# A hybrid attention trunk on one core: a fifth k pair of the output projection as 2x2 block products

## The chip, the core and the metric

One core of a Trainium2 chip runs the whole program. The metric is device time in microseconds (us), the median of three runs. The engines are TensorE (PE in the profile, its weight loads PEld), VectorE (DVE), ScalarE (ACT), GpSimd (POOL) and SyncE (SP), which issues most DMA transfers.

## The reference

Two layers over x of 512 tokens by 2048 features, in float32. Each layer does

```
h = rmsnorm(x, norm_g)
aq, ak, av, ag, bq, bk, bv, bg = split(h @ w_in)         # 2048 x 6400
ya = chunked attention with relative bias (16 heads) * silu(ag)
yb = sliding window attention, rope, sinks (16 heads, 2 kv) * silu(bg)
x  = x + concat(ya, yb) @ w_out                          # 2048 x 2048
```

and a last rmsnorm follows. The change concerns `concat(ya, yb) @ w_out`, mostly, and the tables of rope and bias.

## The kernel before

Everything is kept transposed: features on the 128 partitions, the 512 tokens along the free axis. A projection makes output tiles of 128 features; each sums over 16 k tiles. To keep float32 accuracy with the fast matmul type, each operand is split into a high and a low part, and each product is three matmuls: high weights by high activations, high by low, low by high. ScalarE copies the raw weights into the high part (`hi_place`, or `split_w` in the plain tiles), VectorE subtracts to make the low part (`lo_place`), and TensorE waits for it (`w_lo_done`). The activations' parts are `act_hi` and `act_lo`.

The output projection of a layer has 16 output tiles. Tiles 0 to 3 are made one by one (`project`). From there they are made in pairs, o = 2 to 7 in layer 0 and 2 to 6 in layer 1 (`SUM_FIRST`, `SUM_END`), 11 pairs in all; the last two tiles of layer 1 are plain again. In a pair, the 8 k pairs (two k tiles by two output tiles, a 2x2 block of weights, against the two k tiles of activations, of which each is cut into left and right tokens) are "chunks" of two kinds. A "p" chunk is 12 matmuls of 512 columns (`plain_products`, L800 to L805). An "s" chunk does the 2x2 block product in seven instead of eight products (`sum_products`, L787 to L789): 21 matmuls of 256 columns. It needs sums of weights (`sum_w`, four VectorE ops on 128x128 blocks that make 7 blocks out of 4) and sums of activations. These are made once a layer, in place in `xy` (`sum_y`, four VectorE ops), and split into high (`hi_y_sums`, two ScalarE copies) and low (`lo_y_sums`, two VectorE ops).

`CHUNKS` is the order of the chunks in a pair: s0 s1 p0 s2 s3 p1 p2 p3. The raw, high and low weight buffers hold 32 blocks. `place(i)` says where chunk i lies: the s chunks take turns in two places of 7 blocks, the p chunks have four places of 4 blocks behind them. SyncE's `load_place(l, o, i, lows)` loads a chunk (256 KB) when so many low parts are done; `exchange(l, o)` loads the two residual tiles of a pair and stores two finished tiles of x. At the end of a pair VectorE combines the products (`sum_of_products`, L1604 to L1613) and, once TensorE has finished the pair, adds them and the residual into x (`add_products`, L1619); `residual` (L1559) does that for plain tiles. The squares of the new x are summed up on the side (`square` L1031, `sum_odd` L1687, `sum_even`).

Each engine runs a fixed order of work written by hand, and semaphores tie them. The order around the first pair of a layer is in `out_sums` of ScalarE and of VectorE. At the layer's end, layer 1's tiles 0 and 1 are made with alternating quarters; their inputs are copied by ScalarE while the last pair of layer 0 is still being multiplied, as `rows_done` tells which rows of `act_hi` and which weights are free:

```
if L > 0 and c < PTS - 1:
    act.wait_ge(rows_done, L * ROWS_LAYER - ROWS_OUT + ROWS_IN + 2 + c)
copy(w_hi[:, 1, chunk(c)], w_raw[:, 1, chunk(c)]).then_inc(w_hi_second, 1)
```

`strips` holds the bias of one pair of heads, loaded before each pair of the first mixer (`load_strips`), with one corner set by a memset once at the start; `cos_sb` and `sin_sb` are rope's tables, loaded once and read by GpSimd's `rope`.

## Time and profile before

| what | value |
|---|---|
| median of 3 runs | 1628.84 us (1628.83 to 1628.99) |
| profiled execution | 1628.75 us, of which the span shown is 1627.0 us |
| mean granted TensorE clock | 0.998 |
| TensorE busy | 1615.4 us, 8182 matmuls |
| VectorE, ScalarE, GpSimd busy | 1060.9, 875.2, 93.5 us |
| layer 0's first pair starts (first L787) | 684.28 us |
| layer 1's first pair starts | 1485.93 us |

The profile is of one execution. A time in a timeline is the instruction's start from the span's start; the number behind it is its length. Consecutive instructions of one engine overlap a little in their records, so what an instruction costs its engine is read from start to start. A busy TensorE is a stream of matmuls whose records overlap as well.

### The profile page before, as it was taken

The numbers are of one execution on the slowest core, as the hardware profiler recorded it, in microseconds if no ns is written. First come the engines' busy times: TensorE is split into PE (matmuls) and PEld (weight loads), VectorE is DVE, ScalarE is ACT, GpSimd is POOL, SyncE is SP. The second block draws the span as 40 slices with busy tenths as digits, with TensorE's granted clock in tenths as the row PEclk, the third lists the DMA queues.
The fourth block names the chain that finished last, engine by engine and source line by source line (L and its number), as shares of the span: only waits on it lengthen the run. The fifth ranks groups of instructions, "written<-read, shape, count | busy, mean of one in ns | idle before, by whom it ended". The sixth has DMA issues, their size and how long they took to land.

```text
span 1627.0 us, 23808 instructions
## 1 busy us (share of the span) xinstructions
PE 1615.4 (99%) x8182; PEld 1370.8 (84%) x8182; DVE 1060.9 (65%) x2378; ACT 875.2 (54%) x1907; POOL 93.5 (6%) x74
## 2 busy tenths in 40 slices
PE   9999999999999999999999999999999999999997
PEld 7888888888888888899888888888888888888997
DVE  7655555555577777777755555555556677787765
ACT  7555655555646666333545555655546466653333
POOL 0000000000121200000000000000002212000000
PEclk9999999999999999999999999999999999999999
DMA  7232222232322322444432232222232323223443
GB/s 253 90 104 101 89 78 89 90 115 75 104 93 91 104 98 91 137 145 149 140 129 79 89 115 90 89 77 89 96 109 89 100 91 104 91 91 123 130 136 117
DMA packets 49724, 173.75 MB, mean 107 GB/s; under 512 B 6464, under 2 KB 10848, under 8 KB 35696
## 3 DMA queue, kind: packets, MB, share of 16 engines
q1 hardware_dynamic: 49184, 172.16, 31.6%
q8 instruction: 41, 0.67, 0.2%
q10 hardware_dynamic: 432, 0.55, 0.1%
q14 instruction: 35, 0.29, 0.1%
q0 software_dynamic: 32, 0.08, 0.0%
HBM read 159.58 MB, written 8.47 MB: 103 GB/s over the span
## 4 chain that ended last, share of the span: by engine, by line
PE 99%; DVE 0%; DMA 0%; DVEq 0%; ACT 0%; issue 0%; ACTq 0%
PE ps_proj L581 23%; PE ps_proj L583 23%; PE ps_proj L582 23%; PE ps_o L648 2%; PE ps_t L638 2%; PE ps_o L800 1%; PE ps_o L804 1%; PE ps_o L805 1%; PE ps_proj L800 1%; PE ps_proj L804 1%; PE ps_proj L805 1%; PE ps_s L630 1%; PE ps_s L629 1%; PE ps_o L688 1%; PE ps_s L663 1%; PE ps_o L581 1%
## 5 line engine op out<-in xcount | busy, mean ns | idle before, releaser
L581 PE MATMUL ps_proj<-act_hi,w_hi 128*128 128x512 f32 x1632 | 643.8, 394 | 0.0
L583 PE MATMUL ps_proj<-act_hi,w_lo 128*128 128x512 f32 x1632 | 637.7, 391 | 0.0
L582 PE MATMUL ps_proj<-act_lo,w_hi 128*128 128x512 f32 x1632 | 636.5, 390 | 0.0
L1285 DVE TENSOR_TENSOR w_lo<-w_raw,w_hi 128x512 fp32r<-128x512 f32 (+1 forms) x528 | 380.1, 736 | 176.3 <-ACT w_hi L898 174.1
L898 ACT ACTIVATE w_hi<-w_raw 128x512 fp32r<-128x512 f32 (+1 forms) x528 | 330.9, 649 | 128.3 <-DVE w_raw L1593 61.9
L583 PEld LDWEIGHTS ps_proj<-act_hi,w_lo 128*128 128x128 f32 x1632 | 306.3, 188 | 66.6
L582 PEld LDWEIGHTS ps_proj<-act_lo,w_hi 128*128 128x128 f32 x1632 | 306.9, 188 | 57.4
L581 PEld LDWEIGHTS ps_proj<-act_hi,w_hi 128*128 128x128 f32 x1632 | 306.6, 188 | 57.7
L964 ACT ACTIVATE probs<-probs,nmax 128x128 f32<-128x128 f32 (+3 forms) x128 | 72.1, 563 | 109.8 <-DVE nmax L1357 106.7
L898 ACT ACTIVATE probs<-probs,rden 128x128 f32<-128x128 f32 (+3 forms) x128 | 72.1, 563 | 106.7 <-DVE rden L1378 106.7
L898 ACT ACTIVATE arena<-ps_t 128x512 fp32r<-128x512 f32 (+4 forms) x168 | 74.6, 448 | 68.3 <-PE ps_t L674 50.5
L1285 DVE TENSOR_TENSOR arena<-ps_t,arena 128x512 fp32r<-128x512 f32 (+4 forms) x168 | 85.0, 510 | 37.7 <-ACT arena L898 36.4
L1297 DVE SCALAR_TENSOR_TENSOR temp<-ps_proj,rstd 128x512 f32<-128x512 f32 x94 | 64.5, 686 | 42.5 <-PE ps_proj L583 41.4
L898 ACT ACTIVATE temp<-ps_o 64x256 f32<-64x256 f32 (+1 forms) x96 | 43.3, 451 | 84.6 <-PE ps_o L648 62.2
L1357 DVE CUSTOM_DVE_ANT_0 probs<-ps_s,strips 128x256 f32<-128x256 f32 (+2 forms) x96 | 53.3, 555 | 49.5 <-PE ps_s L630 49.2
L1873 POOL TENSOR_TENSOR temp<-temp,cos_sb 128x512 f32<-128x512 f32 x18 | 24.1, 1338 | 955.2 <-DVE temp L1297 955.2
L1285 DVE TENSOR_TENSOR k_st<-temp,k_st 64x512 fp32r<-64x512 f32 x72 | 52.4, 728 | 31.1 <-ACT k_st L898 30.3
L981 ACT ACTIVATE probs<-probs,nmax 128x128 f32<-128x128 f32 (+1 forms) x128 | 49.1, 384 | 38.6 <-DVE nmax L1371 38.6
L1286 DVE SCALAR_TENSOR_TENSOR arena<-temp,arena 64x512 fp32r<-64x512 f32 x64 | 43.9, 686 | 25.2 <-ACT arena L898 24.2
L898 ACT ACTIVATE arena<-temp 64x512 fp32r<-64x512 f32 x64 | 40.3, 629 | 37.2 <-DVE temp L1297 23.5
L1031 ACT ACTIVATE temp<-xy 128x512 f32<-128x512 f32 x30 | 18.5, 631 | 75.7 <-DVE xy L1619 55.0
L638 PE MATMUL ps_t<-flip_sb,probs 128*128 128x128 f32 x320 | 56.2, 273 | 0.0
(264 smaller groups left out, 2203.1 us busy)
## 6 DMA issues: line engine op xcount, KB each, us to landing
w_raw<-w SPq DMA_DIRECT2D x107, 1024.0 KB, 4.8
w_raw<-w SPq DMA_DIRECT2D x98, 256.0 KB, 3.8
temp<-temp SPq DMA_DIRECT2D x72, 64.0 KB, 4.0
strips<-ext SPq DMA_DIRECT2D x16, 256.0 KB, 5.7
temp<-xT SPq DMA_DIRECT2D x16, 256.0 KB, 4.0
xs<-xy SPq DMA_DIRECT2D x16, 256.0 KB, 3.8
temp<-xs SPq DMA_DIRECT2D x16, 256.0 KB, 2.7
strips<-ext SPq DMA_DIRECT2D x16, 224.0 KB, 5.7
```

What stands on the lines that cost most here:

```text
L581: pe.matmul(dst, wh, act_hi[:, k, :], start=start, stop=False)
L582: pe.matmul(dst, wh, act_lo[:, k, :], start=False, stop=False)
L583: return pe.matmul(dst, wl, act_hi[:, k, :], start=False, stop=stop)
L638: mm = pe.transpose(ps_t[e % 2][:, kt * P:(kt + 1) * P], probs[:, e % 2, kt * P:(kt + 1) * P], flip_sb[:, :])
L648: mm = pe.matmul(ps_o[h][:, kt * P:SEQ], a_v[:, kt, h * P:(h + 1) * P], part[:, kt * (PT_STEP + P):kt * PT_STEP + SEQ], start=(kt == 0 and ...
L898: return nc.scalar.activation(dst, src, ACT.Copy, scale=scale)
L964: nc.scalar.activation(row, row, ACT.Exp, bias=nmax[:, e % 2, 0:1], scale=-1.0, accum_out=psum_e[:, e % 2, 0:1]).then_inc(exp_done, 1)
L981: nc.scalar.activation(row, row, ACT.Exp, bias=nmax[:, n % 2, b:b + 1], scale=-1.0, accum_out=psum_e[:, n % 2, b:b + 1])
L1285: return nc.vector.tensor_tensor(dst, src, hi, ALU.subtract)
L1286: return nc.vector.scalar_tensor_tensor(out=dst, in0=src, scalar=scale, in1=hi, op0=ALU.mult, op1=ALU.subtract)
L1297: nc.vector.scalar_tensor_tensor(out=dst, in0=(ps or ps_proj[s % 2])[:, :], scalar=scale, in1=rstd[:, :], op0=ALU.mult, op1=ALU.mult).then ...
L1357: nc.vector.tensor_tensor_reduce(out=probs[:, e % 2, 0:n], in0=ps_s[e % 2][:, 0:n], in1=bias, scale=-1.0, scalar=LOWEST, op0=ALU.add, op1= ...
```

## The change

Five of the eight k pairs are "s" chunks now (`SUM_K = 5`), and the order in a pair is s0 s1 s2 s3 s4 p0 p1 p2. The s chunks take turns in three places of 7 blocks; p0 and p1 lie behind them, and p2 lies in the third s place, behind its first 3 blocks. So s2's high part waits for the end of the pair before, and p2's for s2's products. The sums of activations of the fifth k pair need room: they take that of `strips`, `cos_sb` and `sin_sb`, which therefore are filled again in layer 1 (two transfers ahead of the first strips, and a memset). `sum_y(4)` and its parts are made within the first pair. At the end of layer 0, all quarters of layer 1's tile 1 are copied after the last pair.

```diff
@@ -61,17 +61,23 @@
 V_LAYER = PAIRS + 1
 ROPES = PAIRS + 1
-ROWS_IN, ROWS_OUT = PTS - 1, 4
+ROWS_IN, ROWS_OUT = PTS - 1, 3
 ROWS_LAYER = ROWS_IN + ROWS_OUT
 SUM_FIRST = 2
 SUM_END = (OUT_TILES // 2, OUT_TILES // 2 - 1)
-SUM_K = 4
-CHUNKS = (("s", 0), ("s", 1), ("p", 0), ("s", 2), ("s", 3), ("p", 1), ("p", 2), ("p", 3))
+SUM_K = 5
+CHUNKS = (("s", 0), ("s", 1), ("s", 2), ("s", 3), ("s", 4), ("p", 0), ("p", 1), ("p", 2))
 BLOCKS = 7 * P
 PLAIN = 4 * P
+N_PLAIN = KT // 2 - SUM_K
+SUM_PLACES = 3
+SUM_TURNS = tuple(len(range(p, SUM_K, SUM_PLACES)) for p in range(SUM_PLACES))
+PLAIN_FIRST = (SUM_PLACES * BLOCKS, SUM_PLACES * BLOCKS + PLAIN, SUM_PLACES * BLOCKS - PLAIN)
 W11, W12, S3, W22, S1, S2, S4 = range(7)
@@ -117,13 +123,17 @@
             return ctx.enter_context(nc.semaphore(name))
+        with nc.sbuf_tensor("strips_tables", [P, 4, SEQ], F32) as strips_tables:
+            strips = strips_tables[:, 0:2, :]
+            cos_sb, sin_sb = strips_tables[:, 2, :], strips_tables[:, 3, :]
+        y_sum_last = sb("y_sum_last", [P, 2, 2, SEQ], F32R)
         act_hi = sb("act_hi", [P, KT, SEQ], F32R)
         act_lo = sb("act_lo", [P, KT, SEQ], F32R)
         xy = sb("xy", [P, KT, SEQ])
         w_raw = sb("w_raw", [P, 2, KT * P])
         w_hi = sb("w_hi", [P, 2, KT * P], F32R)
         w_lo = sb("w_lo", [P, 2, KT * P], F32R)
-        strips = sb("strips", [P, 2, SEQ])
         arena = sb("arena", [P, ARENA], F32R)
         k_st = sb("k_st", [P, 2, 2, SEQ], F32R)
@@ -132,8 +142,6 @@
         temp = sb("temp", [P, 7, SEQ])
         rstd = sb("rstd", [P, SEQ])
         r_cols = sb("r_cols", [P, QT])
-        cos_sb = sb("cos_sb", [P, SEQ])
-        sin_sb = sb("sin_sb", [P, SEQ])
         eye_sb = sb("eye_sb", [P, P])
         flip_sb = sb("flip_sb", [P, P])
         ones_sb = sb("ones_sb", [P, 1])
@@ -248,8 +256,11 @@
         half_done = sem("half_done")
-        sum_in = [sem(f"sum_in{i}") for i in range(2)]
-        plain_in = [sem(f"plain_in{i}") for i in range(4)]
+        sum_in = [sem(f"sum_in{i}") for i in range(SUM_PLACES)]
+        plain_in = [sem(f"plain_in{i}") for i in range(N_PLAIN)]
+        strips_set = sem("strips_set")
+        tables_in = sem("tables_in")
         w_summed = sem("w_summed")
         multiplied = sem("multiplied")
         y_summed = sem("y_summed")
@@ -375,16 +386,19 @@
             kind, n = CHUNKS[i]
             if kind == "s":
-                return slice(n % 2 * BLOCKS, (n % 2 + 1) * BLOCKS)
-            return slice(2 * BLOCKS + n * PLAIN, 2 * BLOCKS + (n + 1) * PLAIN)
+                return slice(n % SUM_PLACES * BLOCKS, (n % SUM_PLACES + 1) * BLOCKS)
+            return slice(PLAIN_FIRST[n], PLAIN_FIRST[n] + PLAIN)
         def block_of(buf, n, b):
-            first = n % 2 * BLOCKS + b * P
+            first = n % SUM_PLACES * BLOCKS + b * P
             return buf[:, first:first + P]
         def y_sum(part, j):
             i, r = divmod(j, 2)
+            if i == 4:
+                return y_sum_last[:, part, r, :]
             buf = (k_f, v_st, arena, arena)[i]
             first = (2048 if i == 3 else 0) + (part * 2 + r) * SEQ
             return buf[:, first:first + SEQ]
@@ -466,8 +480,9 @@
                 sp.wait_ge(w_lo_done, (n - 2) * PTS + lows)
                 kind, c = CHUNKS[i]
                 first = place(i).start
-                sp.dma_start(raw_f[:, first:first + PLAIN], w[n + (kind == "p")][:, c * PLAIN:(c + 1) * PLAIN]
-                             ).then_inc((sum_in[c % 2] if kind == "s" else plain_in[c]), 16)
+                t, q = divmod(c if kind == "s" else SUM_K + c, PTS)
+                sp.dma_start(raw_f[:, first:first + PLAIN], w[n + t][:, q * PLAIN:(q + 1) * PLAIN]
+                             ).then_inc((sum_in[c % SUM_PLACES] if kind == "s" else plain_in[c]), 16)
             def load_out(l):
                 exchange(l, 1)
@@ -475,14 +490,15 @@
                     if o > SUM_FIRST:
                         exchange(l, o - 1)
-                    order = (((0, 4), (1, 4), (2, 8), (5, 8), (6, 8), (7, 8)) if o == SUM_FIRST else
-                             ((2, 3), (0, 4), (1, 5), (5, 6), (6, 7), (7, 8)))
+                    order = (((0, 2), (1, 4), (2, 6), (5, 7), (6, 8)) if o == SUM_FIRST else
+                             ((0, 4), (1, 5), (5, 6), (6, 7), (2, 8)))
                     for i, lows in order:
                         load_place(l, o, i, lows)
                     for par in range(2):
                         sp.sem_inc(w_in[par], 16)
                     load_place(l, o, 3, 9)
                     load_place(l, o, 4, 10)
+                    load_place(l, o, 7, 11)
                 exchange(l, SUM_END[l] - 1)
                 n = tile0(l) + IN_TILES + 2 * SUM_END[l]
                 for s, lows in ((0, 5), (1, 8)):
@@ -532,6 +548,9 @@
                 prefetch(T, 1)
                 for s in range(2, 4):
                     prefetch(T, s)
+                with sp.If(L > 0):
+                    for dst, src in ((cos_sb, cos), (sin_sb, sin)):
+                        sp.dma_start(dst[:, :], src).then_inc(tables_in, 16)
                 sp.wait_ge(ext_out, 16)
                 load_strips(L, 0)
                 with sp.Fori(1, PAIRS) as u:
@@ -799,12 +818,12 @@
                         cols = slice(first + (2 * r + k) * P, first + (2 * r + k + 1) * P)
                         mm = pe.matmul(dst, hi_f[:, cols], act_hi[:, row, :], start=False, stop=False, skip_group_check=True)
-                        if o == OUT_TILES // 2 - 1 and k == 0 and (r == 0 and j > 0 or j == 3):
+                        if o == OUT_TILES // 2 - 1 and k == 0 and r == 0:
                             mm.then_inc(rows_done, 1)
                         pe.matmul(dst, hi_f[:, cols], act_lo[:, row, :], start=False, stop=False, skip_group_check=True)
-                        mm = pe.matmul(dst, lo_f[:, cols], act_hi[:, row, :], start=False, stop=j == 3 and k == 1,
+                        mm = pe.matmul(dst, lo_f[:, cols], act_hi[:, row, :], start=False, stop=j == N_PLAIN - 1 and k == 1,
                                        skip_group_check=True)
-                if j < 3:
+                if j < N_PLAIN - 1:
                     mm.then_inc(multiplied, 1)
                 else:
                     mm.then_inc(proj_done, 2)
@@ -1043,12 +1062,12 @@
                 else:
                     act.wait_ge(plain_in[n], (nth(l, o) + 1) * 16)
-                if i < 3 and o == SUM_FIRST:
+                if i == 2 or i < 2 and o == SUM_FIRST:
                     act.wait_ge(proj_done, tile0(l) + IN_TILES + 2 * o + (i == 2))
-                elif i in (0, 1):
+                elif i < 2:
                     act.wait_ge(multiplied, nth(l, o - 1) * 7 + (4, 5)[i])
-                elif i in (3, 4):
-                    act.wait_ge(multiplied, nth(l, o) * 7 + (1 if i == 3 else 2))
+                elif i in (3, 4, 7):
+                    act.wait_ge(multiplied, nth(l, o) * 7 + {3: 1, 4: 2, 7: 3}[i])
                 copy(hi_f[:, place(i)], raw_f[:, place(i)]).then_inc(w_hi_done, 1)
             def out_sums(l):
@@ -1057,10 +1076,13 @@
                 for i in range(2):
                     hi_place(l, SUM_FIRST, i)
                 for o in range(SUM_FIRST, SUM_END[l]):
+                    hi_place(l, o, 2)
                     if o > SUM_FIRST:
                         square(l + 1, 2 * o - 2, o - 1, 0)
                     square(l + 1, 2 * o - 1, o - 1, 1)
-                    for i in range(2 if o == SUM_FIRST else 3, len(CHUNKS)):
+                    if o == SUM_FIRST:
+                        hi_y_sums(l, 4, 5)
+                    for i in range(3, len(CHUNKS)):
                         hi_place(l, o, i)
                     if o + 1 < SUM_END[l]:
                         hi_place(l, o + 1, 0)
@@ -1070,7 +1092,6 @@
                     copy(w1[:, 0:SEQ // 2], sum_banks(o)[1][0][:, 0:SEQ // 2]).then_inc(p1_copied, 1)
                     if o + 1 < SUM_END[l]:
                         hi_place(l, o + 1, 1)
-                        hi_place(l, o + 1, 2)
                 n = tile0(l) + IN_TILES + 2 * SUM_END[l]
                 act.wait_ge(w_in[0], n * 8 + 16)
                 for c in range(PTS):
@@ -1165,9 +1186,9 @@
                     if L < 1:
                         act.wait_ge(w_first[1][c], 16)
                     if L > 0 and c == 0:
                         act.wait_ge(w_in[1], 8 * TILES + 16)
-                    if L > 0 and c < PTS - 1:
-                        act.wait_ge(rows_done, L * ROWS_LAYER - ROWS_OUT + ROWS_IN + 2 + c)
+                        act.wait_ge(proj_done, T + 1)
                     copy(w_hi[:, 1, chunk(c)], w_raw[:, 1, chunk(c)]).then_inc(w_hi_second, 1)
                     if L < 1:
                         squares_first((c * KC + 1, c * KC + 3))
@@ -1583,7 +1604,7 @@
             def sum_w(l, o, n):
                 done = (nth(l, o) * SUM_K + n) * 4
-                dve.wait_ge(sum_in[n % 2], (nth(l, o) * 2 + n // 2 + 1) * 16)
+                dve.wait_ge(sum_in[n % SUM_PLACES], (nth(l, o) * SUM_TURNS[n % SUM_PLACES] + n // SUM_PLACES + 1) * 16)
                 b = [block_of(raw_f, n, i) for i in range(7)]
                 nc.vector.tensor_tensor(b[S1], b[S3], b[W22], ALU.add).then_inc(w_summed, 1)
                 dve.wait_ge(w_summed, done + 1)
@@ -1629,17 +1650,23 @@
                 sum_w(l, SUM_FIRST, 1)
                 lo_place(l, SUM_FIRST, 0)
                 lo_place(l, SUM_FIRST, 1)
+                sum_w(l, SUM_FIRST, 2)
                 for o in range(SUM_FIRST, SUM_END[l]):
                     if o == SUM_FIRST:
                         residual(l, 3, 1, 1, O + 3)
                         lo_place(l, o, 2)
-                        sum_w(l, o, 2)
+                        sum_y(l, 4)
                     else:
                         add_products(l, o - 1)
+                        lo_place(l, o, 2)
+                    sum_w(l, o, 3)
                     lo_place(l, o, 3)
-                    sum_w(l, o, 3)
+                    if o == SUM_FIRST:
+                        lo_y_sums(l, 4)
+                    sum_w(l, o, 4)
+                    lo_place(l, o, 4)
                     sum_odd(l + 1, 2 * o - 1, o - 1)
-                    for i in range(4, len(CHUNKS)):
+                    for i in range(5, len(CHUNKS)):
                         lo_place(l, o, i)
                     if o + 1 < SUM_END[l]:
                         sum_w(l, o + 1, 0)
@@ -1648,7 +1675,6 @@
                     sum_of_products(l, o)
                     if o + 1 < SUM_END[l]:
                         lo_place(l, o + 1, 1)
-                        lo_place(l, o + 1, 2)
                         sum_w(l, o + 1, 2)
                 n = O + 2 * SUM_END[l]
                 for c in range(PTS):
@@ -1751,6 +1777,8 @@
                     nc.vector.tensor_scalar(nsink[:, :], psink[:, :], -1.0, None, ALU.mult).then_inc(nsink_set, 1)
                     dve.wait_ge(nsink_set, 1)
                 if L > 0:
+                    nc.vector.memset(strips[64:P, :, SEQ - CHUNK:SEQ], NEG).then_inc(strips_set, 1)
+                    dve.wait_ge(strips_set, 1)
                     dve.wait_ge(x_stored, 16 * OUT_TILES)
                     carry_wait(dve)
                 with dve.Fori(1, PAIRS) as u:
@@ -1882,6 +1910,8 @@
             pool.wait_ge(const_in, 16 * N_CONST)
             with pool.Fori(0, DEPTH) as L:
                 B = tile0(L) + A_SLOTS
+                with pool.If(L > 0):
+                    pool.wait_ge(tables_in, 2 * 16)
                 rope(B, t_k, L, 0)
                 rope(B + 1, t_q, L, 1)
                 rope(B + 2, t_k, L, 2)
```

## Rows read from the trace of the kernel before

**Rows 1.** Part 1 of the page: busy time, share, instructions of each engine.

```profile
PE 1615.4 (99%) x8182; PEld 1370.8 (84%) x8182; DVE 1060.9 (65%) x2378; ACT 875.2 (54%) x1907; POOL 93.5 (6%) x74
```

**Rows 2.** What TensorE waited for: us in total, times, longest.

```profile
PE ps_t L838 <- DVE strips L1704: 1.4, 1, 1.4
PE ps_t L581 <- DVE act_lo L1286: 1.2, 1, 1.2
```

**Rows 3.** Timeline of TensorE, layer 0's first pair: start, length, line, tiles, shapes.

```profile
684.28 0.28 PE L787 MATMUL ps_s<-act_hi,w_hi 128*128 128x256 f32 x1
...
686.80 0.28 PE L787 MATMUL ps_s<-act_hi,w_hi 128*128 128x256 f32 x1
...
692.07 0.28 PE L787 MATMUL ps_s<-act_hi,w_hi 128*128 128x256 f32 x1
...
694.58 0.28 PE L787 MATMUL ps_s<-act_hi,w_hi 128*128 128x256 f32 x1
```

**Rows 4.** Timeline of VectorE, a middle pair of layer 0.

```profile
726.48 1.29 DVE L1619 TENSOR_TENSOR xy<-ps_proj,probs 128x512 f32<-128x512 f32 x2 [1.83 <-PE ps_proj L805]
...
740.25 0.42 DVE L1604 TENSOR_TENSOR temp<-ps_s,probs 128x256 f32<-128x256 f32 x1
...
742.91 1.69 DVE L1285 TENSOR_TENSOR w_lo<-w_raw,w_hi 128x896 fp32r<-128x896 f32 x2
...
747.48 1.29 DVE L1619 TENSOR_TENSOR xy<-ps_o,probs 128x512 f32<-128x512 f32 x2 [1.83 <-PE ps_o L805]
```

**Rows 5.** Timeline of VectorE up to and in layer 0's first pair.

```profile
658.48 1.29 DVE L1285 TENSOR_TENSOR k_st<-xy,k_st 128x512 fp32r<-128x512 f32 x2 [0.70 <-ACT k_st L898]
...
659.69 0.42 DVE L1571 TENSOR_TENSOR xy<-xy 128x256 f32<-128x256 f32 x1
...
661.41 0.68 DVE L1559 TENSOR_TENSOR xy<-ps_proj,temp 128x512 f32<-128x512 f32 x1
...
662.24 0.69 DVE L1285 TENSOR_TENSOR w_lo<-w_raw,w_hi 128x512 fp32r<-128x512 f32 x1 [0.15 <-DVE xy L1559]
...
675.36 1.40 DVE L1575 TENSOR_TENSOR xy<-xy 128x256 f32<-128x256 f32 x1
...
684.48 0.69 DVE L1559 TENSOR_TENSOR xy<-ps_proj,temp 128x512 f32<-128x512 f32 x1 [1.05 <-PE ps_proj L583]
...
689.16 1.09 DVE L1285 TENSOR_TENSOR w_lo<-w_raw,w_hi 128x896 fp32r<-128x896 f32 x1 [1.02 <-ACT w_hi L898]
...
690.17 0.28 DVE L1588 TENSOR_TENSOR w_raw<-w_raw 128x128 f32<-128x128 f32 x1
...
691.23 0.69 DVE L1687 TENSOR_TENSOR temp<-temp 128x512 f32<-128x512 f32 x1
...
692.34 2.90 DVE L1285 TENSOR_TENSOR w_lo<-w_raw,w_hi 128x896 fp32r<-128x896 f32 x4 [0.42 <-ACT w_hi L898]
```

**Rows 6.** Timeline of ScalarE in the same stretch.

```profile
657.82 1.15 ACT L898 ACTIVATE k_st<-xy 128x512 fp32r<-128x512 f32 x2 [2.62 <-DVE xy L1577]
...
688.18 0.95 ACT L898 ACTIVATE w_hi<-w_raw 128x896 fp32r<-128x896 f32 x1 [1.81 <-DVE w_raw L1593]
```

**Rows 7.** Timelines at the start of layer 1, and median landing times on the page.

```profile
807.85 2.74 DVE L1286 SCALAR_TENSOR_TENSOR act_lo<-xy,gain_sb,act_hi 128x512 fp32r<-128x512 f32 x4
...
843.41 0.75 SPq L429 DMA_DIRECT2D strips<-ext  x1
...
856.49 0.28 DVE L1353 TENSOR_TENSOR probs<-ps_s,strips 128x128 f32<-128x128 f32 x1
...
w_raw<-w SPq DMA_DIRECT2D x98, 256.0 KB, 3.8
...
strips<-ext SPq DMA_DIRECT2D x16, 256.0 KB, 5.7
```

**Rows 8.** Stretches: us, busy of the engines, granted clock, DMA share, GB/s.

```profile
6.00:8.00 2.00, 0.93 (x9) 0.73 (x7) 1.38 (x3) 1.82 (x3) 0.00 (x0) 1.00 1.01 344
...
1619.00:1620.00 1.00, 0.00 (x0) 0.00 (x0) 1.00 (x2) 0.00 (x0) 0.00 (x0) 0.52 0.00 0
```

## The prediction

> **What bounds the kernel now.** I read the page's busy times first: TensorE works 1615.4 of 1627.0 us [rows 1], so time can only come from fewer or shorter matmuls, and can only be lost where TensorE is made to wait. Then its waits: four in all, the two longest 1.4 and 1.2 us at the very start [rows 2], the other two in the last 25 us. In the output projection, where the change is, there is none. Then its timeline through the first pair of output tiles of layer 0 [rows 3]: the reader is to see two prices in it. A "s" chunk (21 matmuls of 256 columns) takes 686.80 - 684.28 = 2.52 us, 0.120 each. Two "s" chunks and a "p" chunk take 692.07 - 684.28 = 7.79. A whole pair, from the moment VectorE may add one pair's products to the moment it may add the next, takes 747.48 - 726.48 = 21.00 [rows 4]; with four "s" chunks at 2.52 that leaves 10.92 for four "p" chunks, 2.73 each, 0.2275 for each of their 12 matmuls of 512 columns. Last, the timelines of VectorE and ScalarE, which make each chunk's high and low parts just ahead of TensorE [rows 4 to 6]: they are not the bound, but the order in which they work decides whether the fifth "s" chunk is there in time.
>
> **What the change removes.** Per pair of tiles, one "p" chunk becomes an "s" chunk: 2.73 - 2.52 = 0.21 us. There are 6 such pairs in layer 0 and 5 in layer 1: 11 x 0.21 = 2.31 us, 0.14% of the time. The arithmetic falls by one eighth of a chunk (21 x 256 columns for 12 x 512), which would be 12.5% of 2.73 = 0.34; the row gives less because each short matmul costs 0.120, more than half of 0.2275.
> The Trainium skill, "TensorE: Matmul & The Clock Gate", section "Back-to-back issue gap", puts the isolated gap at columns / 2.4 GHz plus about 2.5 ns: 216 and 109 ns, which would be an estimate of 12 x 0.216 - 21 x 0.109 = 0.30 us a pair and 3.3 us in all. The rows measure 0.2275 and 0.120 here, and they decide.
>
> **What it adds, in a middle pair.** A fifth preparation of sums on VectorE (four ops, 691.23 - 690.17 = 1.06 us [rows 5]) and a low part of 896 instead of 512 columns (690.17 - 689.16 = 1.01 against (2.90 - 1.09) / 3 = 0.60). Does VectorE become the bound? I lay out its pair in the new order. Start after the pair's end 0.19; add_products 1.21 and its wait 0.15; five times sums and low part, 5 x 2.07 = 10.35; in three of these it idles while ScalarE copies (0.04 after the sums, and 689.16 - 688.18 = 0.98 from the start of the copy to the low part [rows 5, 6]), 3 x 1.02; sum_odd 0.60; three plain low parts 1.81; sum_of_products 742.91 - 740.25 = 2.66 [rows 4]. Together 20.03 of the pair's new length of 20.79: TensorE stays the bound, by 0.76.
> Are the late chunks in time? Counted from the pair's start, the low part of s2 ends at 2.6; sums, copy and low part of s3 bring it to 5.7, wanted at 3 x 2.52 = 7.56; the same for s4 to 8.8, wanted at 10.08. That is 1.3 to spare, so I cost middle pairs at nothing. s2's high part now waits for the end of the pair before, since p2 lies in its place, and starts at 0.2; it is wanted at 5.04. The transfer into place 0 for the next pair now stands on SyncE's queue behind p2's, which waits for s2's low part at 2.6, and behind the exchange's four: five issues of at most 0.75 (the strips' row) end at 6.4, and with 3.8 us to land [rows 7] it is there at 10.2. VectorE wants it at 11.2. Were it later, VectorE's 0.76 would go first.
>
> **What it adds in the first pair of each layer.** Here sum_y(4), its two high and two low parts are new work between s2 and s4, while chunk p0, which gave 2.73 us of TensorE's time between s1 and s2, has gone behind s4. In before, the low part of s3, fifth in order, ends at 692.34 + 1.09 = 693.43 and TensorE takes it at 694.58 [rows 3, 5]: only 1.15 to spare. The new order on VectorE, from layer 0's rows:
> residual(3) starts at 684.48 as before; ScalarE's copy of s2 waits for the same matmul, starts about 684.54, so the low part of s2 starts at 684.54 + 0.98 = 685.52 (after the residual's 0.83, 662.24 - 661.41), next op 686.53. sum_y(4): 661.41 - 659.69 = 1.72, to 688.25. sum_w(3) 1.06, to 689.31, last op's end 689.37. ScalarE copies s3 from 689.41 (its two copies of y sums, 1.15 from 688.36, end just then); the low part starts 690.39, ends 691.48. Wanted at 684.28 + 7.56 = 691.84: in time by 0.3. lo_y_sums(4) 659.69 - 658.48 = 1.21, from 691.40 to 692.61. sum_w(4) to 693.67, end of its last op 693.74; copy from 693.78; low part from 694.76 to 695.85. TensorE wants s4 at 684.28 + 4 x 2.52 = 694.36 and would get it at 695.85 plus some 0.14 to start: **a stall of 1.63 us**. Layer 1's first pair has the same rows 801.65 later, so it stalls too: 3.26 us. Bounds: 0 (if the queue order gave s4 priority in some way I misread) and 2.63 each, if an op of VectorE in the chain is held for 1 us, as the one at 675.36 is (1.40 for 0.42). I take 1.63, worked out op by op. Behind the stall nothing is late: p0 to p2 get 1.63 more, and the next pair starts with s0 and s1 ready.
>
> **What it moves at the layer's end.** The second tile's chunks of layer 1 are copied only after the last pair, not during it. ScalarE may start 0.2 after the end, and with 0.98 for copy to low part (that of the larger block, so a bound) and 0.69 for the low part, the first is there 1.9 after the end. TensorE first has the 12 matmuls of tile 0, 2.73 us, and their inputs were made in the pair's shadow as in before, where VectorE is at the first rows by 807.85, 2.4 us ahead of the pair's end [rows 7]. Later chunks gain: each takes TensorE 5.46 for both tiles, and VectorE about 3.3. Cost 0; bound 1.
>
> **Tables and strips** are loaded again in layer 1: two 256 KB transfers go ahead of the first strips. Those are issued at 843.41, land 5.7 later and are first read at 856.49 [rows 7]; were the tables' 2 x 3.8 wholly in series in front, they would land at 856.7. Transfers overlap, so I cost 0; bound 0.5. GpSimd's rope reads the tables some 300 us later. The memset and its wait are under 0.3 on VectorE, ahead of a 0.3 idle. The end of the kernel is as before.
>
> **Sum.** -2.31 + 3.26 = +0.95 on the profiled execution, 1628.75 (span 1627.0 and 1.75 around it), so 1629.7; the median of the runs is 1628.84, 0.09 above it: **1629.8 us**. A difference under 0.2%, 3.3 us, can hardly be told from none.
>
> **Rivals.**
> - *The late chunk is hidden*: s4 is in time in the first pairs, or the stall is under 0.5. Then the 2.31 remain: 1626.5, still within 0.2%. For it: the two low parts of y sums (1.21) moved ahead would nearly do. Against it: the chain is serial between two engines, and there are 1.6 us to find. Chance 0.13.
> - *VectorE becomes the bound in all pairs*: it decides when its pair exceeds 20.79, so by 0.76 more than summed; a late transfer into place 0 would do that, repeated. At 21.8, 9 middle pairs cost 1.0 each: 1639. For it, idle of only 0.76; against it, before ran with 1.83 idle [rows 4] and exact 21.00 periods. Chance 0.06.
> - *The clock falls in the stalls.* In the trace it stays at 1.00 in the stretch that holds the wait of 1.2 us [rows 2, 8] and is near half only once TensorE's work is over. If a stall of 1.63 dropped it to 1.2 GHz for 3 us each time, that costs 1.5 twice: 1632.8. Chance 0.07.
> - *More is late once* (s3 too, a held op in the chain, the layer's end, the strips): 1 to 3 more: about 1631.8. Chance 0.14.
> - *Faster by over 0.2%*: needs matmul gaps shorter than rows show, and no stall. 1625.4. Chance 0.05.
>
> The forecast holds with 0.55. Range 1626.0 to 1633.0: from the hidden stall to the fall of the clock. Of the chances, slower by over 0.2% (above 1632.1) are VectorE's, the clock's and a third of "more is late": 0.18; faster 0.05; the same 0.77.
>
> **What would show it.** In the new trace TensorE waits about 1.6 us before the fifth chunk (L787 on the y sums of k rows 8 and 9) once in each layer, released by VectorE's low part; pairs between have a period of 20.79 with no wait; the strips' first use has no wait for a transfer. I am wrong if the first pairs show no wait, if every pair does, or if TensorE waits between the layers.

## The result, and the profile after

The changed kernel takes 1633.99 us, the median of 8 runs (1633.68 to 1634.5), where the kernel before took 1629.05 beside it (8 runs, 1628.71 to 1629.64). It is slower by 4.94 us: ratio 1.003, with a 95% interval of 1.0019 to 1.0041. The profiled execution took 1634.5 us, its span is 1632.7, and the mean granted clock is 0.997. It is the longest of the 8 runs, so below I take differences stage by stage and not from the two spans.

Part 1 of the page after: busy time, share and instructions of each engine. It answers to [rows 1].

```profile
PE 1616.6 (99%) x8281; PEld 1375.1 (84%) x8281; DVE 1092.0 (67%) x2435; ACT 879.0 (54%) x1911; POOL 99.9 (6%) x74
```

VectorE has 31.1 us more. GpSimd has 6.4 us more with the same 74 instructions: it was given no work, so some of its instructions take longer. That is the first sign of what follows.

The waits of TensorE after, which answer to [rows 2]: us in total, times, longest.

```profile
PE ps_s L806 <- DVE w_lo L1306: 3.8, 6, 1.5
PE ps_t L857 <- DVE strips_tables L1730: 1.4, 1, 1.4
PE ps_t L600 <- DVE act_lo L1307: 1.1, 1, 1.1
PE ps_t L806 <- DVE w_lo L1306: 0.6, 3, 0.2
```

L806 is what L787 was, the first matmul of a product of an "s" chunk. Two waits of 1.5 us are the ones forecast for the first pair of each layer. The other seven are not: they stand in middle pairs, where I had forecast none. TensorE's timeline shows both kinds; each group of rows is the last matmul of s3 and the first two of s4, in layer 0's first pair and in two of its middle pairs.

```profile
694.49 0.28 PE L808 MATMUL ps_s<-arena,w_lo 128*128 128x256 f32 x1
696.28 0.36 PE L806 MATMUL ps_s<-act_hi,w_hi 128*128 128x256 f32 x1 [1.51 <-DVE w_lo L1306]
696.48 0.28 PE L807 MATMUL ps_s<-act_lo,w_hi 128*128 128x256 f32 x1
...
717.01 0.28 PE L808 MATMUL ps_t<-arena,w_lo 128*128 128x256 f32 x1
717.42 0.39 PE L806 MATMUL ps_t<-act_hi,w_hi 128*128 128x256 f32 x1
717.64 0.28 PE L807 MATMUL ps_t<-act_lo,w_hi 128*128 128x256 f32 x1
...
759.40 0.28 PE L808 MATMUL ps_t<-arena,w_lo 128*128 128x256 f32 x1
759.86 0.39 PE L806 MATMUL ps_t<-act_hi,w_hi 128*128 128x256 f32 x1 [0.19 <-DVE w_lo L1306]
760.09 0.28 PE L807 MATMUL ps_t<-act_lo,w_hi 128*128 128x256 f32 x1
```

From start to start, matmuls of 256 columns are 0.12 apart. In the first pair the gap is 696.28 - 694.49 = 1.79, so 1.67 are lost there. In the last group it is 0.46, so 0.34, and the first matmul after a wait takes 0.1 longer as well (0.20 and 0.23 for 0.12): 1.75 and 0.44 in all. The middle group has no entry in the list of waits, and still a gap of 0.41. Read through all pairs, the gap ahead of s4 is 0.41 in the first middle pair of each layer and 0.46 to 0.48 in the seven others: all nine are late, not seven.

Why is s4 late there? The timeline of VectorE after, in a middle pair of layer 0:

```profile
749.85 1.28 DVE L1640 TENSOR_TENSOR xy<-ps_o,probs 128x512 f32<-128x512 f32 x2
751.28 1.09 DVE L1306 TENSOR_TENSOR w_lo<-w_raw,w_hi 128x896 fp32r<-128x896 f32 x1
752.29 1.38 DVE L1609 TENSOR_TENSOR w_raw<-w_raw 128x128 f32<-128x128 f32 x1
753.71 0.29 DVE L1611 TENSOR_TENSOR w_raw<-w_raw 128x128 f32<-128x128 f32 x1
...
756.56 0.29 DVE L1609 TENSOR_TENSOR w_raw<-w_raw 128x128 f32<-128x128 f32 x1
...
758.72 1.09 DVE L1306 TENSOR_TENSOR w_lo<-w_raw,w_hi 128x896 fp32r<-128x896 f32 x1 [1.02 <-ACT w_hi L917]
...
771.08 1.28 DVE L1640 TENSOR_TENSOR xy<-ps_proj,probs 128x512 f32<-128x512 f32 x2
```

One row stands out. The op of L1609 takes 0.29 at 756.56 and 1.38 at 752.29: it is held for 1.1 us. L1640, which in [rows 4] stood behind an idle time of 1.83, has none left, and comes 771.08 - 749.85 = 21.23 after the one before it. TensorE needs 20.79 for the pair. The timeline of GpSimd after, beside it:

```profile
751.64 1.89 POOL L1894 TENSOR_TENSOR temp<-temp 128x512 f32<-128x512 f32 x1 [19.33 <-ACT temp L1050]
```

It is the add of `sum_even`, which sums the squares of the new x; it becomes free when ScalarE has made the square of the even tile. It stands once in every pair, and in every middle pair it meets the same op of VectorE. In the kernel before, GpSimd and VectorE were these:

```profile
675.16 1.31 POOL L1866 TENSOR_TENSOR temp<-temp 128x512 f32<-128x512 f32 x1 [11.61 <-ACT temp L1031]
...
728.04 1.30 POOL L1866 TENSOR_TENSOR temp<-temp 128x512 f32<-128x512 f32 x1 [19.70 <-ACT temp L1031]
```

```profile
730.04 1.09 DVE L1285 TENSOR_TENSOR w_lo<-w_raw,w_hi 128x896 fp32r<-128x896 f32 x1 [2.27 <-ACT w_hi L898]
```

There the add of a middle pair, 728.04 to 729.34, fell wholly into VectorE's idle time of 2.27 us. The other one, at 675.16, met an op of `sum_y`: that is the one at 675.36 in [rows 5] that took 1.40 for 0.42.

The two stages of pairs give the whole sum. Timelines of TensorE, after and then before: the first matmul of the pairs of layer 0 and their last one, the first matmul of the pairs of layer 1 and the first behind them. The rows missing here from before are at 684.28 [rows 3] and 1485.93.

```profile
684.54 0.28 PE L806 MATMUL ps_s<-act_hi,w_hi 128*128 128x256 f32 x1
...
812.90 0.39 PE L824 MATMUL ps_proj<-act_hi,w_lo 128*128 128x512 f32 x1
...
1488.77 0.28 PE L806 MATMUL ps_s<-act_hi,w_hi 128*128 128x256 f32 x1
...
1596.12 0.28 PE L783 MATMUL ps_proj<-act_hi,w_hi 128*128 128x256 f32 x1
```

```profile
810.06 0.39 PE L805 MATMUL ps_proj<-act_hi,w_lo 128*128 128x512 f32 x1
...
1590.93 0.28 PE L764 MATMUL ps_proj<-act_hi,w_hi 128*128 128x256 f32 x1
```

In layer 0, from start to start, it is 812.90 - 684.54 = 128.36 for 810.06 - 684.28 = 125.78; in layer 1 it is 1596.12 - 1488.77 = 107.35 for 1590.93 - 1485.93 = 105.00. That is 2.58 + 2.35 = 4.93 us, and the medians differ by 4.94. Between the layers, from 812.90 to 1488.77 and from 810.06 to 1485.93, the distance is 675.87 in both kernels, so nothing is lost at the layer's end or by the tables.

### The profile page after: what moved, and what is told of

Same layout as the page of the kernel before. It is cut to its first block, busy times and chain, and to the rows that moved or that the text cites. A ratio compares the mean times of both kernels' runs of the same rounds, so it can differ in the third digit from the quotient of the medians.

```text
span 1632.7 us, 24098 instructions
## 1 busy us (share of the span) xinstructions
PE 1616.6 (99%) x8281; PEld 1375.1 (84%) x8281; DVE 1092.0 (67%) x2435; ACT 879.0 (54%) x1911; POOL 99.9 (6%) x74
## 4 chain that ended last, share of the span: by engine, by line
PE 84%; DVE 11%; ACT 2%; issue 1%; DMA 0%; DVEq 0%; SPq 0%; ACTq 0%
PE ps_proj L600 22%; PE ps_proj L602 22%; PE ps_proj L601 22%; DVE w_lo L1306 4%; PE ps_o L667 2%; PE ps_t L657 2%; ACT w_hi L917 2%; DVE w_raw L1609 1%; PE ps_s L649 1%; PE ps_s L648 1%; DVE w_raw L1611 1%; PE ps_o L707 1%; PE ps_s L682 1%; PE ps_o L600 1%; PE ps_o L602 1%
## 5 line engine op out<-in xcount | busy, mean ns | idle before, releaser
L1306 DVE TENSOR_TENSOR w_lo<-w_raw,w_hi 128x512 fp32r<-128x512 f32 (+1 forms) x528 | 387.9, 748 | 172.3 <-ACT w_hi L917 168.7
L917 ACT ACTIVATE w_hi<-w_raw 128x512 fp32r<-128x512 f32 (+1 forms) x528 | 335.4, 656 | 198.1 <-DVE w_raw L1614 137.4
L1378 DVE CUSTOM_DVE_ANT_0 probs<-ps_s,strips_tables 128x256 f32<-128x256 f32 (+2 forms) x96 | 53.3, 555 | 49.3 <-PE ps_s L649 48.9
L1901 POOL TENSOR_TENSOR temp<-temp,strips_tables 128x512 f32<-128x512 f32 x18 | 24.1, 1340 | 949.1 <-DVE temp L1318 949.1
L1306 DVE TENSOR_TENSOR k_st<-temp,k_st 64x512 fp32r<-64x512 f32 x72 | 53.4, 742 | 31.1 <-ACT k_st L917 30.3
L917 ACT ACTIVATE k_st<-temp 64x512 fp32r<-64x512 f32 x72 | 45.3, 630 | 14.1 <-DVE temp L1318 13.5
```

Source lines behind the costliest of these rows:

```text
L917: return nc.scalar.activation(dst, src, ACT.Copy, scale=scale)
L1306: return nc.vector.tensor_tensor(dst, src, hi, ALU.subtract)
L1378: nc.vector.tensor_tensor_reduce(out=probs[:, e % 2, 0:n], in0=ps_s[e % 2][:, 0:n], in1=bias, scale=-1.0, scalar=LOWEST, op0=ALU.add, op1= ...
```

## The experiments

The theories. **A**: GpSimd's add holds VectorE's next op for about 1.1 us, VectorE's pair becomes longer than TensorE's, and that costs some 0.4 us in each of nine middle pairs; the stall in the first pairs is a second, separate loss. **B**: VectorE is late for another reason (a transfer, its own work, the clock), and the long op is an effect or costs nothing. The runs of the kernel before beside each experiment had medians between 1628.89 and 1629.06.

**The even sum on VectorE** (`e1_even_on_vector`). The add of the middle pairs is made by VectorE itself, behind its own odd one; this gives it 0.60 us more work, and GpSimd has no add left there that could hold it. GpSimd keeps the adds outside the middle pairs; that part of the edit is not shown.

```
                     sum_odd(l + 1, 2 * o - 1, o - 1)
+                    if o > SUM_FIRST:
+                        dve.wait_ge(sq_done, (l + 1) * KT + 2 * o - 1)
+                        dve.wait_ge(acc_done[0], (l + 1) * (KT // 2) + o - 1)
+                        nc.vector.tensor_tensor(acc[0], acc[0], sq[0], ALU.add).then_inc(acc_done[0], 1)
```

> The changed kernel with the sum of even squares of the middle pairs (sum_even, one add of 128x512) made by VectorE right after sum_odd, and not by GpSimd; nothing else changes. Theory A, GpSimd's add holds VectorE's first op of sum_w(3) for 1.10 us in each middle pair: the hold goes, the new op costs VectorE 0.60, its pair takes 20.03 + 0.60 = 20.63, TensorE is the bound again at 20.79 and waits for s4 in no middle pair; 9 x (21.22 - 20.79) = 3.9 us less than the changed kernel's 1634.0, so 1630.1. Theory B, the op is held by something that comes with its place (its instruction, the transfers of the exchange): the 1.10 stays, VectorE's pair becomes 21.8 and the time 1634.0 + 9 x 0.6 = 1639. The stalls of 1.5 in the first pairs stay under both.

Measured: 1630.13 us (1629.76 to 1630.8), ratio to before 1.0008 (0.9999 to 1.0017). Of the waits before L806 only the two long ones of the first pairs are left:

```profile
PE ps_s L806 <- DVE w_lo L1306: 3.0, 2, 1.5
```

In the middle pairs TensorE waits no more, though VectorE has more work of its own than in the changed kernel. Behind the stall VectorE's rows of L1640 are 20.73 apart, 0.1 more than the 20.63 expected, until TensorE's 20.78 is the longer one. A holds, B falls. By the difference of medians against before, 1630.13 - 1628.89 = +1.24 is left: -2.31 and two stalls.

**The sums of y made early** (`e2_y_sums_early`). `sum_y(4)` and its parts are made together with those of the fourth k pair, ahead of the first pair of output tiles. Their old places, not shown, are dropped.

```
 def out_sums(l):                       # ScalarE
+    hi_y_sums(l, 3, 5)
     square(l + 1, 2, 1, 0)
-    hi_y_sums(l, 3, 4)
...
 def out_sums(l):                       # VectorE
-    residual(l, 2, 1, 0, O + 2)
     sum_y(l, 3)
+    sum_y(l, 4)
     lo_y_sums(l, 3)
+    lo_y_sums(l, 4)
+    residual(l, 2, 1, 0, O + 2)
```

> The changed kernel with sum_y(4) and its high and low parts made together with those of sum_y(3), ahead of residual(2), where VectorE had nothing to do for 3 us; nothing is left out. Theory: the stall before s4 in the first pair of each layer is the new work between s2 and s4 and goes; TensorE has no wait there. Each stall cost 1.79 - 0.12 = 1.67 us, so 1634.0 - 3.3 = 1630.7. Rival: the work in front now makes s0 or s1 late, or the hold of VectorE by GpSimd falls into the chain, and 1 us a layer comes back: 1632.7. The 0.43 of the middle pairs stays under both.

Measured: 1630.38 us (1629.82 to 1630.86), ratio 1.0009 (1.0 to 1.0018). The waits of 1.5 us are gone, the seven short ones of the middle pairs stay:

```profile
PE ps_s L806 <- DVE w_lo L1304: 0.8, 4, 0.2
PE ps_t L806 <- DVE w_lo L1304: 0.6, 3, 0.2
```

So the two losses are separate: this edit takes back 1633.99 - 1630.38 = 3.6, and the one before it 3.9.

**Both** (`e3_both`): the edits of the last two in one kernel.

> Both edits at once. If the two causes are all that stands between the changed kernel and the sum of the matmuls, pairs take 20.79, TensorE has no wait in the output projection, and the time is 1634.0 - 3.9 - 3.3 = 1626.8, that is 2.3 us (11 x 0.21) under before's 1629.05. If a third cause is there (layer's end, tables, strips), it is longer by that.

Measured: 1626.72 us (1626.32 to 1626.94), ratio 0.9986 (0.9977 to 0.9995). No wait before L806 is left, and VectorE's pairs follow TensorE's again, 767.62 - 746.85 = 20.77 apart here and 20.78 on average:

```profile
746.85 1.29 DVE L1638 TENSOR_TENSOR xy<-ps_o,probs 128x512 f32<-128x512 f32 x2
...
767.62 1.29 DVE L1638 TENSOR_TENSOR xy<-ps_proj,probs 128x512 f32<-128x512 f32 x2
```

The gain of the shorter matmuls, forecast as 2.31, is measured here alone: 1628.89 - 1626.72 = 2.17.

**GpSimd's add twice, after and before** (`e4_pool_twice`, `e5_before_pool_twice`). A second add of the same shape, into a tile that is free then, ahead of the real one: once in the changed kernel, once in the kernel before.

```
 with pool.Fori(1, OUT_TILES // 2 - 1) as o:
+    pool.wait_ge(sq_done, (L + 1) * KT + (o * 2 + 1))
+    nc.gpsimd.tensor_tensor(rstd[:, :], sq[0], sq[0], ALU.add)
     sum_even(L + 1, o * 2, o)
```

> The changed kernel with a second add of 128x512 on GpSimd ahead of sum_even's, of the same squares into a free tile; the result is not used. Theory A (GpSimd's add holds VectorE's ops that read two tensors of SBUF): VectorE is held about another 1.1 to 1.3 us in each middle pair, 9 x 1.1 to 1.3 = 10 to 12 us more, 1644 to 1646, with pairs of 22.3 to 22.5. Theory B (the held op is held by something else): no change, 1634.0.

> The kernel before, with the same second add of 128x512 on GpSimd as in the run e4. Theory A says that GpSimd's add costs nothing in before only because it falls where VectorE waits (2.27 us for ScalarE's copy after add_products, 1.83 at the pair's end): the second add ends some 0.5 after the low part of s2 wants to start, which is held by about 0.5 to 1.0; VectorE's 1.83 at the pair's end takes it up, periods stay at 21.00, time within 1 us of before. Rival: the hold reaches TensorE in before as well, and the time rises by 5 us or more, as in e4.

Measured, in the changed kernel: 1641.64 us (1641.53 to 1641.85), ratio 1.0078 to before (1.0063 to 1.0094). The direction is A's, the size is not: 1641.64 - 1633.99 = 7.65 more, where A expected 10 to 12, and 0.72 a pair (21.94 for 21.22) for 1.1 to 1.3. The timelines of VectorE and of GpSimd in this kernel show why:

```profile
753.40 1.09 DVE L1306 TENSOR_TENSOR w_lo<-w_raw,w_hi 128x896 fp32r<-128x896 f32 x1
754.41 1.13 DVE L1609 TENSOR_TENSOR w_raw<-w_raw 128x128 f32<-128x128 f32 x1
755.58 1.26 DVE L1611 TENSOR_TENSOR w_raw<-w_raw 128x128 f32<-128x128 f32 x1
756.76 0.28 DVE L1612 TENSOR_TENSOR w_raw<-w_raw 128x128 f32<-128x128 f32 x1
```

```profile
753.64 1.75 POOL L1923 TENSOR_TENSOR rstd<-temp 128x512 f32<-128x512 f32 x1 [18.89 <-ACT temp L1050]
755.36 1.33 POOL L1894 TENSOR_TENSOR temp<-temp 128x512 f32<-128x512 f32 x1
```

The engines take turns, one instruction each: the first op is held 0.85, gets its turn, and the next is held 0.97, together 1.82 where one add held 1.10. So the second add costs 0.72 a pair, 9 x 0.72 = 6.5. Part of why it is not 1.10 is that the new add, which reads one tile twice, is the shorter one: 1.04 alone, as the kernel before shows below, for 1.30. The rest lies in the first pairs: from the first matmul to `add_products` they take 23.57 for 22.87, 0.70 more in each layer, because s3 now starts 0.5 late too. Together that is 6.5 + 1.4 = 7.9, for 7.65 by the medians.

In the kernel before, the second add costs nothing: 1629.1 us (1628.76 to 1629.61), ratio 1.0 (0.999 to 1.0009). I had expected a hold of 0.5 to 1.0 to be seen on the low part of s2, with room for it; there is hardly one. Timelines of GpSimd and of VectorE:

```profile
749.17 1.04 POOL L1893 TENSOR_TENSOR rstd<-temp 128x512 f32<-128x512 f32 x1 [18.71 <-ACT temp L1031]
750.17 1.29 POOL L1866 TENSOR_TENSOR temp<-temp 128x512 f32<-128x512 f32 x1
```

```profile
751.30 1.12 DVE L1285 TENSOR_TENSOR w_lo<-w_raw,w_hi 128x896 fp32r<-128x896 f32 x1 [2.27 <-ACT w_hi L898]
```

Two adds in a row end at 751.46 by the record, and the low part that starts at 751.30 takes 1.12 for 1.09: both fit into the idle 2.27. That the middle pairs of this kernel can bear a hold was not tested by it. Ahead of layer 0's first pair it does hold VectorE more, in two ops of `sum_y(3)`, by 0.72 and 0.98 where the kernel before has 0.98 once [rows 5], and there is time for it:

```profile
675.62 1.14 DVE L1575 TENSOR_TENSOR xy<-xy 128x256 f32<-128x256 f32 x1
676.80 1.40 DVE L1577 TENSOR_TENSOR xy<-xy 128x256 f32<-128x256 f32 x1
```

**A collision in the kernel before** (`e8_before_even_collides`). So I moved ScalarE's square of the even tile behind its copy of the third "s" chunk, s2, which puts the add onto `sum_w(3)` there too. Nothing else is changed but the counts of squares that `sum_odd` and GpSimd wait for, which are not shown.

```
 for o in range(SUM_FIRST, SUM_END[l]):
-    if o > SUM_FIRST:
-        square(l + 1, 2 * o - 2, o - 1, 0)
     square(l + 1, 2 * o - 1, o - 1, 1)
     for i in range(2 if o == SUM_FIRST else 3, len(CHUNKS)):
         hi_place(l, o, i)
+        if o > SUM_FIRST and i == 3:
+            square(l + 1, 2 * o - 2, o - 1, 0)
```

> The kernel before with ScalarE's square of the even tile moved behind the high part of s2, so that GpSimd's add falls on VectorE's sum_w(3) instead of VectorE's idle time. Theory A: one op of VectorE is held by 0.7 to 1.1 us in each middle pair, visible as 1.0 to 1.4 instead of 0.28, and it costs no time, since VectorE has 1.83 us idle at the end of the pair: periods 21.00, time within 1 us of before. Rival (s3, wanted 1.15 us after it was ready in before's first pair, is made late by the hold, so that idle at the pair's end does not help): periods up to 21.5, 3 to 5 us more.

Measured: 1629.11 us (1628.71 to 1629.62), ratio 1.0001 (0.9991 to 1.001). Timelines of GpSimd and of VectorE in it:

```profile
751.79 1.59 POOL L1866 TENSOR_TENSOR temp<-temp 128x512 f32<-128x512 f32 x1 [19.41 <-ACT temp L1031]
```

```profile
726.58 1.29 DVE L1619 TENSOR_TENSOR xy<-ps_proj,probs 128x512 f32<-128x512 f32 x2 [0.72 <-PE ps_proj L805]
...
752.15 1.38 DVE L1588 TENSOR_TENSOR w_raw<-w_raw 128x128 f32<-128x128 f32 x1
```

The same hold of 1.1 us is there, once a pair. It is taken from the idle time at the pair's end, 0.72 where [rows 4] have 1.83, and the time stays. The collision costs nothing by itself; it costs where VectorE has less than 1.1 us to spare.

**The square late in the changed kernel** (`e6_square_late`). ScalarE makes the even square at the pair's end (the counts that follow from it are not shown), so that GpSimd's add falls onto `sum_of_products`, whose first ops each take one input from PSUM (`ps_s`, `ps_t`).

```
 act.wait_ge(multiplied, nth(l, o) * 7 + 5)
 copy(w1[:, 0:SEQ // 2], ...).then_inc(p1_copied, 1)
+if o + 1 < SUM_END[l]:
+    act.wait_ge(w_summed, (nth(l, o + 1) * SUM_K + 2) * 4)
+if o > SUM_FIRST:
+    square(l + 1, 2 * o - 2, o - 1, 0)       # no longer at the pair's start
```

> The changed kernel with GpSimd's add kept and only its time moved: ScalarE squares the even tile of a middle pair just ahead of the high part of the next pair's s1, so that GpSimd's add runs beside sum_of_products, whose first four ops read one tensor from PSUM and one from SBUF. Theory A in its narrow form (only ops with two tensors in SBUF are held): these four are not held, the two adds of the residual at most 0.5; VectorE's pair takes 20.03 to 20.53, so periods are 20.79 and the time is 1634.0 - 3.9 = 1630.1, like e1. In its wide form (every op of VectorE is held while GpSimd works) the hold stays 1.1, the periods stay 21.2, the time 1634.0.

Measured: 1630.18 us (1629.79 to 1630.77), ratio 1.0005 (0.9996 to 1.0014). Timelines of GpSimd and of VectorE:

```profile
744.63 1.30 POOL L1896 TENSOR_TENSOR temp<-temp 128x512 f32<-128x512 f32 x1 [19.44 <-ACT temp L1050]
```

```profile
744.16 0.43 DVE L1629 TENSOR_TENSOR probs<-ps_s,temp 128x256 f32<-128x256 f32 x1
744.50 0.41 DVE L1630 TENSOR_TENSOR probs<-ps_s,temp 128x256 f32<-128x256 f32 x1
744.84 0.41 DVE L1632 TENSOR_TENSOR probs<-ps_s,probs 128x256 f32<-128x256 f32 x1
745.17 1.90 DVE L1636 TENSOR_TENSOR probs<-probs,temp 128x512 f32<-128x512 f32 x2
```

The add runs from 744.63. The two ops at 744.50 and 744.84, with one input in PSUM, keep their 0.41 beside it, and the add keeps its 1.30. The first op with both inputs in SBUF is held: 1.90 for the two of L1636, which take 1.28 elsewhere. That hold of 0.62, for at most 0.5 expected, just fits: VectorE's rows behind the stall are 20.73 to 20.74 apart, for TensorE's 20.78.

**Both remedies without extra work** (`e7_early_square_late`): the edits of `e2_y_sums_early` and `e6_square_late` together.

> e6 with the sums of y of the fifth k pair made early, as in e2. With both stalls gone and VectorE 0.3 to 0.8 us under the pair's length (e3: 0.16), 1626.8 as e3. If the time is the same as e3's, VectorE's spare time is worth nothing more and the kernel is at TensorE's own rate again.

Measured: 1626.59 us (1626.42 to 1626.84), ratio 0.9983 (0.9974 to 0.9992), with no wait before L806. Of the 0.3 to 0.8 us that I expected VectorE to have to spare there is about 0.05 (20.78 - 20.73), and it is enough. It and `e3_both` beat both kernels, by 2.2 to 2.5 us against before and 7.3 to 7.4 against the changed one.

## Why the prediction was wrong

The forecast was +0.95 us and 1629.8, within 0.2%; it came to +4.94, slower, outside the range. Step by step:

- **What is removed: right.** 11 x 0.21 = 2.31 was forecast. A pair takes 20.78 on average between VectorE's rows in `e3_both`, for 21.00, and the medians gave 2.17 there and 2.45 in `e7_early_square_late`. The spacing of the short matmuls that the rows showed was a sound price.
- **The first pair of each layer: right.** A stall of 1.63 before s4 was worked out op by op; it is 1.67, in both layers, with some 0.1 for a slower first matmul behind it. `e2_y_sums_early` removed it.
- **The middle pairs: wrong, and this is the step that failed.** I laid VectorE's pair out as 20.03 of 20.79 and wrote "so I cost middle pairs at nothing". Each op in that list had its free duration, as if VectorE were alone. Its own work is 21.22 - 1.10 = 20.12, and `e1_even_on_vector` gives 20.73 - 0.60 = 20.13, so the list was right to 0.1; what it left out is 1.10 us in which GpSimd's add holds it. 20.12 + 1.10 is above 20.79 by 0.43, and nine middle pairs make 3.9. s4, which I had 1.3 ahead of time, is 0.34 late. The hold is 1.10 of that; 0.2 is that VectorE, now the bound, begins the pair later (749.85, where the pair's first matmul at 749.45 and my 0.19 give 749.64); some 0.3 is what my count from the pair's start was short by.
- **The layer's end, tables and strips: right.** Costed at nothing, and the distance between the layers is 675.87 in both kernels.
- **The clock in the stalls: right.** The granted clock is 1.00 in the stretch 684 to 697, which holds a stall of 1.67, in the stretch 1488 to 1502 with the other one, and around the short waits at 717 and 759. The 3 us at 1.2 GHz by which that rival was priced stood on no row. The mean of 0.997 for 0.998 comes from the kernel's end, as told below.

The sum with the forecast gain and the measured losses: -2.31, 2 x (1.67 + 0.08) and 9 x 0.43 give -2.31 + 3.50 + 3.87 = +5.06, for 4.94 measured. With 2.17 or 2.45, the gain as the medians gave it, it is 5.2 or 4.9.

The rival "VectorE becomes the bound in all pairs" is what happened in the nine middle pairs, and its point of decision, a pair 0.76 longer than summed, was right: 1.1 is more. But I named a late transfer as the only thing that could bring it, gave it 0.06, and priced it with 1.0 for each pair instead of 0.43. The rows had the cause in view. The op at 675.36 [rows 5] took 1.40 for 0.42, and I used it as an unexplained hold, for the first pair only. Had I looked at what the other engines did at that time, GpSimd's row at 675.16 would have explained it; and had I followed the square that ScalarE makes at a pair's start, I would have found the add falling onto work instead of idle time, because the change moves low part and sums into the 2.27 us where it used to run.

The Trainium skill, "SBUF — State Buffer", section "Who interferes with whom", has the rule that I did not weigh: a VectorE instruction with two inputs in SBUF and a GpSimd instruction that reads SBUF exclude each other, and whichever comes first keeps the shared ports for its whole length. The runs agree at each point that they test: 1.10 of hold (`e8_before_even_collides` and the changed kernel), none on ops with one input in PSUM (`e6_square_late`), and turns of whole instructions (`e4_pool_twice`).

Two differences of the profiled executions lie outside the pairs, and neither comes from the change. Behind layer 1's last pair the kernel after takes 1632.7 - 1596.12 = 36.58, for 1627.0 - 1590.93 = 36.07. TensorE's last four matmuls hold it all, first after, then before:

```profile
1623.21 1.23 PE L771 MATMUL ps_o<-eye_sb,r_cols 128*128 128x128 f32 x4 [0.55 <-DVE r_cols L1844]
```

```profile
1618.02 0.71 PE L752 MATMUL ps_o<-eye_sb,r_cols 128*128 128x128 f32 x4 [0.55 <-DVE r_cols L1816]
```

From 1623.5 to 1624.5 the granted clock is 0.50, the lower of its two levels (1.2 of 2.4 GHz); before, from 1618 to 1619, it is 1.00, and it falls behind these matmuls. In both, TensorE had waited 0.55 just ahead of them. `e6_square_late` has the low clock there too (1.22), the eight other profiled executions have 0.71, those of the changed kernel's variants among them, so it belongs to the execution. The other difference, 0.26 ahead of layer 0's first pair, is scatter as well: that pair starts at 684.54 in `e5_before_pool_twice` too, where TensorE's work up to there is that of the kernel before, and at 684.38 in `e8_before_even_collides`.

## What to carry to other kernels

When an engine's work is laid out to see whether it still fits, its sum of free durations is not enough: list what GpSimd does in the same period, find where it falls now and where the change will put it, and add a hold where it meets a VectorE op with both inputs in SBUF (here 1.10 for an add of 1.30). An op in the trace that takes three times its usual length is a price and not noise; look at the other engines at that time before using it as a bound. Here the cure was not less work but another place for it: the add where VectorE reads PSUM, and once-a-layer work in the time ahead of the loop.

## What the runs showed of the hardware

- The hold goes both ways. GpSimd's add of 128x512 takes 1.30 in the record when alone, 1.59 in `e8_before_even_collides` and 1.89 in the changed kernel, where it starts while the low part at 751.28 is still running. The record of a blocked instruction includes its wait, so a GpSimd instruction that has grown is a sign of a collision.
- The hold ends before the record of the add does: in the changed kernel the add ends at 751.64 + 1.89 = 753.53, and the held op, which needs 0.29, at 753.67, so it ran from 753.38, 0.15 earlier. In `e6_square_late` it is 0.14.
- Two adds back to back (`e4_pool_twice`) hold two ops of VectorE, one each, and not one for the sum of both: 0.85 and 0.97.
- A kernel's last matmuls can run at either clock: four of 128 columns, behind a wait of 0.55, take 0.71 at a granted clock of 1.00 and 1.23 in the profiled execution after, where it had fallen to 0.50 to 0.57.
- The first matmul after a wait of 0.2 to 1.5 us takes 0.20 to 0.23 from start to start for 0.12, at an unchanged granted clock; a short wait costs TensorE some 0.1 more than it shows.
